# Trainium2: waits moved by one turn, heads spaced nine turns apart and three early value loads in the token mix of a hybrid decoder step

## The reference

```python
x = x + 0.5 * swiglu(rmsnorm(x, norm_ffn1), ffn1_w_in, ffn1_w_out)      # D_MODEL 1024, D_FF 2816
p = rmsnorm(x, norm_mix) @ w_in_mix                                     # q, f, i, g | q, k, v, forget
o_a, s_fin = hgrn2(a_q, a_f, a_i, a_g, lb, gain, state0)                # 4 heads, state 128 x 128
logf = log_sigmoid(f_f + f_bias)                                        # per token and FoX head
o_f  = headnorm(attend(q, k, v, logf))                                  # 8 heads of 64
#   prompt: causal softmax(q k^T * scale + cum(logf)_q - cum(logf)_k) v
#   new tokens: the same over 2048 cached rows (16 pages of 128 by page_table) and the 4 new rows
x = x + concat(o_a, o_f) @ w_out_mix
x = x + 0.5 * swiglu(rmsnorm(x, norm_ffn2), ffn2_w_in, ffn2_w_out)
y = rmsnorm(x, norm_final)
```

## Time and profile before

| what | value |
| --- | --- |
| median of the runs | 1329.96 us |
| profiled execution, its own time | 1327.93 us |
| span in its trace | 1326.2 us |
| PE busy | 1280.3 us, 97% of the span |
| DVE, ACT, POOL busy | 605.5, 457.1, 102.4 us |
| mean granted clock of PE | 0.99 |
| first turn of the mix | 589.4 us from the span's start |
| first product of the output projection | 863.5 us |

### The profile page before, as it was taken

The page is one execution under the profiler, slowest core; times in us unless marked ns, Lnnn a source line. Parts: engine busy times, 40 slices in busy tenths (PEclk is TensorE's granted clock), DMA queues, the critical chain, the costliest instruction groups (busy, mean ns, idle before and its releaser), DMA issues.

```text
span 1326.2 us, 29769 instructions
## 1 busy us (share of the span) xinstructions
PE 1280.3 (97%) x12453; PEld 1187.1 (90%) x12453; DVE 605.5 (46%) x1057; ACT 457.1 (34%) x710; POOL 102.4 (8%) x115
## 2 busy tenths in 40 slices
PE   9999999999999999988889889899999999999997
PEld 8999999999999999985546556499999999999997
DVE  6744422443454433337676566554544322334433
ACT  6534311222223113524446556633322211222322
POOL 1000000000022000004333101013000000000000
PEclk9999999999999999998989999999999999999998
DMA  7242322223322442147899888523322422233301
GB/s 196 79 111 78 128 80 63 80 79 103 119 80 64 118 136 75 51 147 241 284 312 320 316 317 297 173 65 96 96 82 76 142 80 64 64 95 103 94 26 68
DMA packets 192023, 172.33 MB, mean 130 GB/s; under 512 B 11393, under 2 KB 155298, under 8 KB 191938
## 3 DMA queue, kind: packets, MB, share of 16 engines
q1 hardware_dynamic: 191730, 170.61, 40.9%
q0 software_dynamic: 144, 0.52, 0.1%
q10 hardware_dynamic: 64, 0.02, 0.0%
HBM read 162.19 MB, written 8.93 MB: 129 GB/s over the span
## 4 chain that ended last, share of the span: by engine, by line
PE 90%; DVE 4%; issue 2%; ACT 1%; DMA 1%; SPq 0%; POOL 0%; ACTq 0%; DVEq 0%
PE ps L2047 75%; PE ps L1071 2%; PE ps L983 2%; PE ps L1090 2%; PE ps L908 1%; PE ps L746 1%; PE ps L948 1%; PE ps L928 1%; PE ps L864 1%; DMA d_keys<-in_cache_k 1%; PE ps L2170 0%; DVE h_totals L1457 0%; DMA gain_rows<-in_norm_final 0%; DVE w_lo L2375 0%; PE ps L783 0%
## 5 line engine op out<-in xcount | busy, mean ns | idle before, releaser
L2047 PE MATMUL ps<-n_hi,w_hi 128*128 128x272 f32 x1856 | 387.1, 288 | 2.0 <-DVE w_lo L2501 0.8
L2047 PE MATMUL ps<-n_hi,w_lo 128*128 128x272 f32 x1856 | 386.7, 288 | 0.0
L2047 PE MATMUL ps<-n_lo,w_hi 128*128 128x272 f32 x1856 | 385.2, 288 | 0.0
L2221 ACT ACTIVATE w_hi<-w_raw 128x2048 fp32r<-128x2048 f32 (+2 forms) x77 | 157.9, 2051 | 540.2 <-PE ps L2047 540.2
L2047 PEld LDWEIGHTS ps<-n_hi,w_hi 128*128 128x128 f32 x1856 | 292.9, 188 | 2.8 <-issue 2.6
L2047 PEld LDWEIGHTS ps<-n_lo,w_hi 128*128 128x128 f32 x1856 | 292.7, 189 | 0.0
L2047 PEld LDWEIGHTS ps<-n_hi,w_lo 128*128 128x128 f32 x1856 | 290.7, 189 | 0.0
L2375 DVE TENSOR_TENSOR w_lo<-w_raw,w_hi 128x2048 fp32r<-128x2048 f32 (+2 forms) x77 | 196.2, 2548 | 49.5 <-ACT w_hi L2221 49.5
L2047 PE MATMUL ps<-g_hi,w_lo 128*128 128x272 f32 x704 | 145.7, 288 | 0.0
L2047 PE MATMUL ps<-g_hi,w_hi 128*128 128x272 f32 x704 | 145.5, 288 | 0.0
L2047 PE MATMUL ps<-g_lo,w_hi 128*128 128x272 f32 x704 | 145.1, 288 | 0.0
(11 more groups left out here) (350 smaller groups left out, 1240.2 us busy)
## 6 DMA issues: line engine op xcount, KB each, us to landing
w_raw<-in_ffn_w_in SPq DMA_DIRECT2D x87, 512.0 KB, 5.0
d_keys<-in_cache_k SPq DMA_DIRECT2D x128, 256.0 KB, 4.6
d_values<-in_cache_v SPq DMA_DIRECT2D x124, 256.0 KB, 5.4
w_raw<-in_w_in_mix SPq DMA_DIRECT2D x28, 512.0 KB, 4.7
w_raw<-in_ffn_w_out SPq DMA_DIRECT2D x16, 768.0 KB, 5.4
w_raw<-in_ffn_w_out SPq DMA_DIRECT2D x16, 640.0 KB, 4.9
w_raw<-in_w_out_mix SPq DMA_DIRECT2D x8, 512.0 KB, 4.7
suffix_scratch<-d_log_f_sums SPq DMA_DIRECT2D x32, 64.0 KB, 2.1
```

Source lines behind the costliest of these rows:

```text
L2047: mm = pe.matmul(bank(4 * j + 2 * t + half), wp, xp[:, k, half * HALF:(half + 1) * HALF], start=(k == 0 and wp is w[0] and xp is x_hi), st ...
L2221: nc.scalar.activation(w_hi[j][:, 0:kt * UC], w_raw[j][:, 0:kt * UC], ACT.Copy).then_inc(w_hi_ready, 1)
```

## The change

Ten edits are made at once, and all of them are in the mix.

1. **Heads nine turns apart**: `HEAD_AT` = 2 + 9i. The copies of the gated outputs (L1378, L1821) move a turn back with it.
2. **Outputs three turns later**: `OUT_AT` = 8b + 22 for six batches; the last two stay at 67 and 70. Their waits change to the weights of the following batch.
3. **Probabilities of the first half a turn later**: PE's L1040 and ACT's copies behind it go from `i` = 6 to `i` = 7. PE's wait there becomes the copies of the outputs (`oF_done`), and L1029 loses that wait except at the end. The first half of `d_out` is copied at 8b + 15 instead of 8b + 13.
4. **State sums first**: DVE's L1567 becomes the first thing in its turn (`state_sums_vector`).
5. **Zeroing on POOL**: six memsets go from DVE to POOL, and PE's wait for them at turn 0 is dropped.
6. **Forget chain**: its first part runs ahead of everything on DVE and is one instruction shorter, the rest goes from turn 1 to turn 2 behind the head's level.
7. **Row tables** (L1401 to L1414) go from turn 2 to the input projection, behind the gates.
8. **Turn 3 on PE**: `rows_tensor` goes behind `products_tensor`.
9. **The copy of `s_v_nat`** on ACT goes from turn 1 to turn 0, ahead of the forget exponentials.
10. **Three value pairs and the first batch's page numbers** are loaded as soon as the last weights of the input projection are issued. The other three follow at turns 5 to 7 (six at turns 4 to 9 before). The forget tiles move to other weight slots.

```diff
-        HEAD_AT = [2 + 8 * i for i in range(H_HG)]
+        HEAD_AT = [2 + 9 * i for i in range(H_HG)]
...
-        fx_z, fx_t, fx_lf = (at(f"forget_{n}", [H_FX, T], F32, G_AT[i]) for i, n in enumerate(("z", "t", "log")))
+        fx_z, fx_t, fx_lf = (at(f"forget_{n}", [H_FX, T], F32, G_AT[3 + i]) for i, n in enumerate(("z", "t", "log")))
-        lf_nat = at("lf_nat", [P, TT + 1, H_FX], F32, G_AT[5])
+        lf_nat = at("lf_nat", [P, TT + 1, H_FX], F32, G_AT[5] + 4 * T)
...
+        def batch_pages(sp, b, pages):
+            _, pages[b] = nc.values_load_multi_w_load_instructions(
+                page_row[0:1, ds(b * PAGES, PAGES)], engines=(mybir.EngineType.SP,), min_val=0, max_val=N_POOL - 1)
         def key_set(sp, n, pages):
-            if s == 0:
-                _, pages[b] = nc.values_load_multi_w_load_instructions(
-                    page_row[0:1, ds(b * PAGES, PAGES)], engines=(mybir.EngineType.SP,), min_val=0, max_val=N_POOL - 1)
+            if s == 0 and b:
+                batch_pages(sp, b, pages)
...
         def mix_sync(sp, load_out):
+            batch_pages(sp, 0, pages)
+            for w in range(3):
+                value_pair(sp, w, pages)
...
-                if 4 <= x < 4 + V_RING:
-                    if x == 4 + 5:
+                if 5 <= x < 5 + V_RING - 3:
+                    if x == 5 + 2:
-                    value_pair(sp, x - 4, pages)
+                    value_pair(sp, x - 2, pages)
...
-                pe.wait_ge(fx_step, 7)
+                pe.wait_ge(fx_step, 6)
...
-                if b >= 2:
-                    pe.wait_ge(oF_done, 2 * (b - 1))
+                if b == DB:
+                    pe.wait_ge(oF_done, 2 * (DB - 1))
-            if i == 6 and b < DB:
+            if i == 7 and b < DB:
-                if b:
-                    pe.wait_ge(w_step, 2 * b)
+                if b == 1:
+                    pe.wait_ge(w_step, 2)
+                elif b:
+                    pe.wait_ge(oF_done, 2 * (b - 1))
...
-                    if c < DB - 1:
+                    if c < DB - 2:
+                        pe.wait_ge(w_step, 2 * c + 4)
+                    elif c < DB - 1:
...
-        OUT_AT = [8 * b + 19 for b in range(DB - 1)] + [70]
+        OUT_AT = [8 * b + 22 for b in range(DB - 2)] + [67, 70]
...
-                rows_tensor(pe, x)
-                if x == 0:
-                    pe.wait_ge(d_zero, 4)
-                    pe.wait_ge(f_ready, 2 * H_HG)
+                if x != 3:
+                    rows_tensor(pe, x)
+                if x == 3:
+                    rows_tensor(pe, x)
...
-            if x == 1:
+            if x == 0:
...
-            if i == 6 and b < DB:
+            if i == 7 and b < DB:
...
-        COPY_AT = [(8 * b + 13, 8 * b + 17) for b in range(DB - 1)] + [(67, 69)]
+        COPY_AT = [(8 * b + 15, 8 * b + 17) for b in range(DB - 1)] + [(67, 69)]
         def forget_scalar(act, x):
+                act.wait_ge(fx_step, 2)
+                nc.scalar.activation(fx_t[:, :], fx_t[:, :], ACT.Exp).then_inc(fx_step, 1)
-                nc.scalar.activation(fx_t[:, :], fx_t[:, :], ACT.Exp).then_inc(fx_step, 1)
-                act.wait_ge(fx_step, 4)
         def mix_scalar(act, split_hi):
-                states_scalar(act, x)
+                if x:
+                    states_scalar(act, x)
+                if x == 0:
+                    states_scalar(act, x)
-                if 42 <= x < 46:
-                    i = x - 42
+                if 43 <= x < 47:
+                    i = x - 43
...
         def forget_vector(dve, x):
-            if x == 0:
-                dve.wait_ge(ff_ready, 1)
-                nc.vector.tensor_scalar(fx_z[:, :], ffT[:, :], f_bias[:, 0:1], None, ALU.add).then_inc(fx_step, 1)
-                dve.wait_ge(fx_step, 1)
-                nc.vector.tensor_scalar(fx_t[:, :], fx_z[:, :], -1.0, None, ALU.mult).then_inc(fx_step, 1)
-                dve.wait_ge(fx_step, 2)
-                nc.vector.tensor_tensor(fx_t[:, :], fx_t[:, :], fx_z[:, :], ALU.min).then_inc(fx_step, 1)
-            if x == 1:
-                dve.wait_ge(fx_step, 5)
+            if x == 2:
+                dve.wait_ge(fx_step, 4)
-                dve.wait_ge(fx_step, 6)
+                dve.wait_ge(fx_step, 5)
+        def row_tables_vector(dve):
+            nc.vector.tensor_copy(d_e8[:, :].rearrange("k (a h) -> k a h", h=H_FX),
+                                  ident[0:H_FX, 0:H_FX].rearrange("k (o h) -> k o h", o=1)
+                                  .to_broadcast([H_FX, P // H_FX, H_FX])).then_inc(dc_step, 1)
+            nc.vector.tensor_reduce(d_selx[:, :], ident[:, :].rearrange("p (a h) -> p a h", h=H_FX), AX_X, ALU.add)\
+                .then_inc(dc_step, 1)
+            nc.vector.tensor_reduce(d_row[:, :], ident[:, :].rearrange("p (g r) -> p r g", r=NR), AX_X, ALU.add)\
+                .then_inc(dc_step, 1)
+            nc.vector.memset(d_nb[:, :], NEG).then_inc(dc_step, 1)
+            nc.vector.memset(d_mx[:, :], NEG).then_inc(dc_step, 1)
+            nc.vector.memset(d_ls[:, :], 0.0)
+            dve.wait_ge(dc_step, 5)
+            nc.vector.tensor_reduce(d_sel[:, :], d_selx[:, :].rearrange("p (g t) -> p t g", t=DS_), AX_X, ALU.add)\
+                .then_inc(dc_step, 1)
+            nc.vector.tensor_copy(d_rows[:, :].rearrange("p (g r) -> p g r", r=NR),
+                                  d_row[:, :].rearrange("p (o r) -> p o r", o=1).to_broadcast([P, 4, NR]))\
+                .then_inc(dc_step, 1)
         def rows_vector(dve, x):
-            if x == 2:
...
+        def state_sums_vector(dve, x):
+            for hb in range(2):
+                h = x - STATE_AT[hb] - 1
+                if 0 <= h < H_HG:
+                    dve.wait_ge(s_pe.sem, s_pe.after(f"st{hb}{h}"))
+                    dve.wait_ge(s_pool.sem, s_pool.after(f"dec{hb}{h}"))
+                    flat = s_S0[:, h, :, :].rearrange("k b v -> k (b v)")
+                    nc.vector.tensor_tensor(flat, flat, ps[:, B_D, :], ALU.add).then_inc(s_dve.sem, 1)
...
-            for hb in range(2):
-                h = x - STATE_AT[hb] - 1
-                if 0 <= h < H_HG:
-                    went(f"S{hb}{h}", f"st{hb}{h}")
-                    dve.wait_ge(s_pool.sem, s_pool.after(f"dec{hb}{h}"))
-                    flat = s_S0[:, h, :, :].rearrange("k b v -> k (b v)")
-                    nc.vector.tensor_tensor(flat, flat, ps[:, B_D, :], ALU.add).then_inc(s_dve.sem, 1)
...
         def mix_vector(dve, split_lo):
+            dve.wait_ge(ff_ready, 1)
+            nc.vector.tensor_scalar(fx_z[:, :], ffT[:, :], f_bias[:, 0:1], None, ALU.add).then_inc(fx_step, 1)
+            dve.wait_ge(fx_step, 1)
+            nc.vector.scalar_tensor_tensor(fx_t[:, :], fx_z[:, :], -1.0, fx_z[:, :], ALU.mult, ALU.min).then_inc(fx_step, 1)
-            for n in range(2):
-                nc.vector.memset(d_q[n][:, :], 0.0).then_inc(d_zero, 1)
-                nc.vector.memset(d_pTn[n][:, :], 0.0).then_inc(d_zero, 1)
-            for n in range(2):
-                nc.vector.memset(h_sc[n][:, :], 0.0).then_inc(sc_zero, 1)
+                state_sums_vector(dve, x)
+                levels_vector(dve, x)
-                levels_vector(dve, x)
...
-                if 44 <= x < 48:
-                    i = x - 44
+                if 45 <= x < 49:
+                    i = x - 45
...
         def mix_gpsimd(pool):
+            for n in range(2):
+                nc.gpsimd.memset(d_q[n][:, :], 0.0).then_inc(d_zero, 1)
+                nc.gpsimd.memset(d_pTn[n][:, :], 0.0).then_inc(d_zero, 1)
+            for n in range(2):
+                nc.gpsimd.memset(h_sc[n][:, :], 0.0).then_inc(sc_zero, 1)
...
+            row_tables_vector(dve)
```

16 lines of the change are left out of this document (removed).

## The result

The changed kernel takes **1311.93 us** (median of four runs, 1309.4 to 1315.15) against 1330.42 for the kernel before in the same session: a ratio of 0.986, 95% interval [0.982, 0.990]. Run again later beside other kernels it took 1309.05 (five runs, 1307.73 to 1312.56), ratio 0.9846 [0.9823, 0.987]. The forecast was 1315.9, range 1307 to 1326. It holds, but the gain is 18.5 to 21 us where the sum gave 14.1.

A forecast was written before the change was run, and what follows sets the result against it. PE was taken as the bound, with transfers as second limit. 5.2 + 8.5 + 1.7 + 1.5 - 0.5 - 2.3 = 14.1 us off the profiled 1327.9 gave 1313.8, or 1315.9 us on the median's scale; range 1307 to 1326.

The forecast's parts named there:

- The opening: Turns 0 to 6: 3.5 us off DVE's chain plus one half-clock stretch of 1.7, 5.2 us saved, bounds 2.1 and 7.1.
- The POOL rival: Opening: memsets on POOL hold DVE up for the 1.4 us they took; 12.7 us saved in all, 1317.3; chance 0.07.
- the sign that the prediction named for a wrong opening: Opening: DVE's first forget steps and `h_k` taking over twice their 0.4 us each.
- The moved waits: Turns 7 to 62: of 11.9 us of PE waits at L1040, L1054, L864, L772, 8.5 go; bounds 5 and 11.9.
- The clock term: Half-clock stretches behind vanished waits go: 1.7 us in the opening; 1.7 in turns 7 to 62, there between 0 and 5.1.
- The turns around 42: PE's 3.7 us wait for `d_keys` at turn 42 is partly filled by moved head products: 1.5 us, between nothing and 3.7.
- Transfers: Less time per turn for SyncE and DMA makes late sets later: 2.3 us cost, between 0 and 7.
- The `oF_done` wait: PE's new wait for DVE's eight copies, mostly covered except in short turns: 0.5 us cost, bounds 0 and 4.8.
- DVE takes the waits' place: Pauses at L1040, L864 or L1054 return at L746, clock stretches stay: 7.0 us saved, 1323; chance 0.18.
- Moves no time: Waits only shadow the transfer rate, so PE arrives earlier and waits for keys: 1329; chance 0.10.
- SyncE falls behind: Page-number reads every eighth turn make each of six batches pay turn 42's price: 16 us slower, 1346; chance 0.06.
- More than that: All 11.9 us of waits, 7.1 in the opening, three clock stretches (5.1), less costs: 21.3 us saved, 1308.7; chance 0.14.

The follow-up runs named there:

- The profile of the early pairs: Kernel before, with only three value pairs and the first page numbers loaded behind the last projection weights: 1329.68 us, ratio 0.9988 (twelve runs).
- edit 1 alone: Kernel before, with only the heads set nine turns apart instead of eight: 1319.33 us, ratio 0.9912 (six runs).
- the state sums alone: Kernel before, with only the state sums made DVE's first work of a turn: 1331.73 us (one run).
- three kernels that take the wait or the memsets to another place: Changed kernel with states reloaded head by head, with state products two turns later, or with those and memsets on DVE: 1315.97, 1315.16, 1315.97 us.
- without the opening: Changed kernel with row tables, forget steps, memsets and the other parts of edits 5 to 9 undone: 1316.41 us, ratio 0.9906 (eight runs).
- the later products: Changed kernel with the products that read the second group of decode states two turns later, load unmoved: 1315.16 us, ratio 0.9898 (six runs).
- the kernel that reloads head by head: Changed kernel with each head's decode states reloaded once its own are stored, products one turn later: 1315.97 us, ratio 0.9905 (six runs).
- edit 3 without it: Kernel before, with only outputs three turns later and first-half probabilities one turn later: 1323.31 us, ratio 0.9943 (nine runs).

## Why the forecast held, point by point

**The opening: 5.2 forecast, 5.5 measured** at turn 7 in the second profile, 4.2 in the first, which has a half-clock stretch at 594.2 that the other profiles with this opening on POOL lack. Taken out of the whole it is worth 5.8 us (1316.5 - 1310.7 in the means). The profile of the early pairs separates the two parts: at full clock the opening takes 24.96 us with the old order and 21.12 with the new one, 3.8 us for the waits and DVE's chain where the sum had 3.5, and the two stretches are the other 1.7. The sum had that too, but as the price of one of them; both are gone, and together they cost what one was put at (at full clock PE waits 1.0 us more there for DVE's picks). The POOL rival had its mechanism right (0.98 us against 0.37), and the sign that the prediction named for a wrong opening, over twice the 0.4 us, came true for `forget_z` and not for `h_k` (0.41). Its price was too high, 0.8 of 1.42 us, and the sum stayed.

**The moved waits and the clock: 8.5 + 1.7 us forecast for turns 7 to 62.** The waits fell as listed. L1054 went from 3.7 to 0.3, L1040 from 3.9 to 0.4, L864 and L772 from 2.9 and 2.7 to no entry (1.1 us of `issue` at L870). Turn 14 kept its pause, now at L752:

```profile
641.56 0.46 PE L752 MATMUL ps<-h_q,h_k 128*32 128x32 f32 x32 [1.65 <-DVE h_scores L1467]
```

That is 1.65 us where 1.1 was worked out. Picks took 3.0 us in all, within the 1 to 4 named. Over all causes PE waited 8.9 and 11.0 us less in the two profiles, and the table leaves 10.4 us as the part at equal clock. The forecast without its two clock terms was 14.1 - 3.4 = 10.7. The three agree.

**The clock term was mis-sized: 3.4 us forecast (1.7 in the opening, 1.7 behind), some 8.7 by the regression.** By this estimate it is the step that makes the difference between 14.1 and 19. The traces go the same way: three stretches fewer in the first profile and five in the second are worth at most 5.1 and 8.5 us, and with 8.9 and 11.0 us less of waits that is 14.0 and 19.5, where the spans fell by 12.8 and 18.0. Its bounds, 0 to 5.1 in the middle, counted only stretches that a named wait preceded, and they counted them in one profile. That profile was one of the better runs: its mean clock is 0.990, eight stretches with the two at the end, against 0.986 and eleven on average. With the change, runs have some seven fewer (25.5 us at half clock less), where only two were counted. On the scale of the profile, 1327.93 before, the forecast was 1313.8, and the two profiled executions of the changed kernel took 1315.15 and 1310.01.

**The turns around 42.** The wait for `d_keys` is 3.4 and 3.2 us, in the 3 to 8 named. Turn 41 fell from 5.66 to 3.86 and 3.58 us: 1.8 to 2.1, for the 1.5 forecast. The turn behind it, at half clock before, fell from 3.22 to 2.48.

**Transfers: 2.3 us forecast as a cost, wrong in place.** Keys are waited for less than before, 3.4 and 3.2 us in place of 4.6; what cost is the states' reload at turn 18, 2.5 and 1.7 us, and a half-clock stretch behind it in the first profile. Together the waits for transfers grew by 1.3 and 0.3 us, where the two terms for them came to 2.3 - 1.5 = 0.8. That the total is near is partly luck, since the wait that makes it was in neither term. The prediction's text on SyncE looked for its stop at the page numbers and missed the one for the stores, which stood in the trace before as a 4.2 us pause of its queue. So turns 7 to 41 did not come down as named: the stretch that was 132.6 us is 127.9 and 127.1 us to the same place in turn 41, not 120 to 124. The clock (0.97 and 0.99) is as named, the DMA share (0.90 and 0.91) at the edge of what was named.

**The `oF_done` wait: 0.5 forecast, 0.4 measured** (L1048). But the exponentials of the second half, L1024, are waited for 2.2 us. The forecast missed that. It is there with edit 1 alone (2.2 us) and not in the kernel without it, so it comes with the nine turns.

**Rivals.** "DVE takes the waits' place" fell: DVE's waits halved. "Moves no time" and "SyncE falls behind" as a loss fell, though a late SyncE, by another stop than that rival named, is what turn 18 now shows. "More than that" (1308.7) had the price nearly right, 1309.05 in the second session lies beside it, but not the terms: the opening did not give 7.1, and turn 14 kept its pause. The medians stand between it and the forecast.

**Why the parts do not add up.** Alone the four bring 10.2 + 6.6 + 5.0 + 0.4 = 22.2 us, together with edit 4 they bring 19.1. Three kernels with one part alone already run into the states' transfer (waits of 1.1, 2.1 and 3.1 us; 1.2 with the state sums alone), and the whole pays it once. The intervals are each 3 to 4 us wide, so a small part of the difference can be chance.

**What stays open.** Why three kernels that take the wait or the memsets to another place run at a lower clock (0.9915 to 0.9933) than the changed one (0.9956); the trace shows the stretches, not what sets them. The profiles with the heads alone, without the opening and with the later products each have 6.8 us at half clock between 844 and 856, behind turn 62, which neither the kernel before nor the changed one has. A second tile for the states, which would take SyncE's stop away altogether, was not tried; the full transfers of the kernel that reloads head by head (1.08) speak against a large gain.

## What to carry to other kernels

Size a clock term with the mean clock of all the runs beside the stretches of one profile: the profile may be one of the better ones. Where PE is to arrive earlier, go through every pause of the queue that issues the transfers, also those that cost nothing yet; a wait for stores ahead of a reload can come onto the path, to use the data later does not help if other loads are queued behind it, and to reload earlier does not help where the transfer engines are full. Moves of single waits are worth more together than a trial of each shows, or less: edit 4 alone moved its wait to the next line, edit 3 without it left L864 at 3.5 us, and only with both was it gone.

## What the hardware showed beside

**A pause that no wait names.** In the first profile a group of L934 stops for 1.04 us within its 32 matmuls, at a clock of 1.00, with its operands there:

```profile
763.84 0.62 PE L934 MATMUL ps<-v_nat,probT 128*32 128x64 f32 x27
765.50 0.31 PE L934 MATMUL ps<-v_nat,probT 128*32 128x64 f32 x5 [1.04 <-issue]
```

The second profile of the same program has none at this place:

```profile
761.61 0.62 PE L934 MATMUL ps<-v_nat,probT 128*32 128x64 f32 x32
```

Turn 48 takes 4.76 us in the first and 3.42 in the second profile, turn 50 takes 5.05 and 3.47. The kernel before has both long (4.50 and 4.79). The two turns are 2.9 of the 5.2 us between the two profiles. What it is was not found.

**The same memset on two engines.** Two `h_scores` memsets of 128x512 took 0.99 us on POOL and 1.02 us on DVE.

**Issue to landing.** The four loads of states were issued from 649.86 and waited for until 656.18, 6.3 us for 1 MB. The DMA engines were busy to 0.36 from 650 to 652 and to 0.99 from there to 656.18, with the page loads behind in the same queue.
